# A mixture of experts on one core: gate/up rows taken eight to a partition, gathers from the plain rows, places by falling number of rows

## The reference, cut to what matters

```
def swiglu(x, w_gu, w_down):
    gate, up = jnp.split(x @ w_gu, 2, axis=-1)
    return (jax.nn.silu(gate) * up) @ w_down
...
        tok, wt, ex = inp
        y = swiglu(x_pad[tok], w_gu[ex], w_down[ex])
        return acc.at[tok].add((y * wt[:, None]).astype(acc.dtype)), None
```

## Time and profile before

| | |
|---|---|
| median of 3 runs | 2564.52 us (2564.05 to 2569.41) |
| the profiled execution | 2562.0 us, span of the trace 2560.0 us |
| PE busy, of the span | 2439.3 us (95%) |
| DVE, ACT, POOL busy | 900.5, 423.2, 793.3 us |
| moved by DMA | 391.36 MB in 167964 packets |
| places and spill loop | about 1677 to 2512 us of the span |

### The profile page before, as it was taken

One profiled execution on the slowest core, in us unless ns is written; L12 is line 12 of the kernel. 1 busy time (PEld: TensorE's weight loads), 2 busy tenths in 40 slices (PEclk: granted clock), 3 DMA queues, 4 the chain that ended last, 5 costly groups with the idle time before them and its releaser, 6 DMA issues. The chain is left out here.

```text
span 2560.0 us, 26577 instructions
## 1 busy us (share of the span) xinstructions
PE 2439.3 (95%) x10446; PEld 1480.8 (58%) x10446; DVE 900.5 (35%) x1540; ACT 423.2 (17%) x665; POOL 793.3 (31%) x764
## 2 busy tenths in 40 slices
PE   6999999999999999999999999979999999999991
PEld 3444554345799544444445544457777777776761
DVE  5011553675533532323323262222222223323325
ACT  1001122335454110010001110001111111111110
POOL 3000111101343100000001135326666666676642
PEclk9999999999999999999999999989999999999996
DMA  6201003100000211111050501079999999999995
GB/s 250 90 33 45 22 33 104 41 17 9 1 1 26 91 49 49 32 43 49 25 206 25 188 30 50 26 291 349 343 343 345 347 345 349 342 345 347 348 321 165
DMA packets 167964, 391.36 MB, mean 153 GB/s; under 512 B 19706, under 2 KB 40234, under 8 KB 167072
## 3 DMA queue, kind: packets, MB, share of 16 engines
q1 hardware_dynamic: 135248, 300.64, 32.2%
q0 software_dynamic: 31584, 82.00, 12.3%
q10 hardware_dynamic: 1008, 7.02, 0.7%
HBM read 322.50 MB, written 67.11 MB: 152 GB/s over the span
## 5 line engine op out<-in xcount | busy, mean ns | idle before, releaser
L1856 PEld LDWEIGHTS banks<-arena 128*128 128x128 f32 x4096 | 523.8, 192 | 75.8 <-DMA arena<-in_exp_w_gu 39.4
L1856 PE MATMUL banks<-arena 128*128 128x128 f32 (+7 forms) x4096 | 533.8, 292 | 30.8 <-DMA arena<-in_exp_w_gu 28.4
L2276 POOL DMA_INDIRECT arena<-hp_scratch,arena x306 | 294.8, 964 | 243.6 <-issue 80.2
L1380 PE MATMUL banks<-arena 128*128 128x512 f32 x672 | 291.8, 594 | 1.3 <-PEq L736 1.3
L328 PE MATMUL banks<-arena 128*128 128x512 f32 x640 | 280.9, 596 | 4.6 <-DVE arena L1093 4.3
L1864 PE MATMUL banks<-arena 128*128 128x512 f32 (+1 forms) x528 | 237.4, 592 | 1.4 <-DVE arena L2240 0.9
L1380 PEld LDWEIGHTS banks<-arena 128*128 128x128 f32 x672 | 127.8, 190 | 163.1 <-issue 163.1
L328 PEld LDWEIGHTS banks<-arena 128*128 128x128 f32 x640 | 120.0, 190 | 159.4 <-issue 149.7
L280 POOL TENSOR_SCALAR arena<-arena 128x1 f32<-128x1 f32 x16 | 15.5, 970 | 604.6 <-DVE arena L271 604.6
L2291 POOL DMA_INDIRECT acc_scratch<-arena x99 | 153.7, 1552 | 66.8 <-DMA acc_scratch<-arena 42.1
L321 PE MATMUL banks<-arena 128*128 128x512 f32 x384 | 168.4, 597 | 0.6 <-PE banks L321 0.6
(11 more groups left out here) (364 smaller groups left out, 2517.4 us busy)
## 6 DMA issues: line engine op xcount, KB each, us to landing
arena<-in_exp_w_gu SPq DMA_DIRECT2D x64, 2048.0 KB, 24.6
arena<-in_exp_w_down SPq DMA_DIRECT2D x64, 1024.0 KB, 20.2
arena<-in_w_in SPq DMA_DIRECT2D x10, 2048.0 KB, 9.3
arena<-in_w_in SPq DMA_DIRECT2D x12, 1024.0 KB, 6.2
arena<-in_w_branch SPq DMA_DIRECT2D x12, 512.0 KB, 7.2
hp_scratch<-arena SPq DMA_DIRECT2D x10, 512.0 KB, 2.9
arena<-hp_scratch,arena POOLq DMA_INDIRECT x306, 6.3
arena<-in_x SPq DMA_DIRECT2D x4, 1024.0 KB, 14.8
```

The costliest lines, as they stand in the source:

```text
L1380: last = nc.tensor.matmul(PS[:, g % 4, :], lhs[:, k, :], rhs[:, k, :], start=(k == 0), stop=(k == 3))
L1856: last = nc.tensor.matmul(PS[:, bank + part, f * n:(f + 1) * n], weights[:, k, part * FF + f * P:part * FF + (f + 1) * P], x[:, k, 0:n], s ...
L2276: nc.gpsimd.indirect_dma_start(out=rows[0:n, :], out_offset=None, in_=table, in_offset=bass.IndirectOffsetOnAxis(ap=at, axis=0)).then_inc( ...
```

## The change

- The gate/up matrix is loaded with rows 8p to 8p + 7 on partition p. They follow each other in memory, 16 KB in one piece.
- The token's row then needs no permutation: quarter q of the plain row, read with the eight numbers of a partition together, fits. The gathers read `hx_scratch`; the permuted copies, their stores, waits and the scratch `hp_scratch` go.
- DVE's transposes read each 32 x 32 block with a step of 8 numbers (32 bytes) from one to the next, where they read neighbours before. In the spill loop PE's eight transposes read with the same step.
- `place_order` sorts by falling capacity: 216, 216, 192, 192, 176 x4, 168 x8, 152 x8, 144 x8, 136 x4, and then all 27 single places; the spill loop stays last.

```diff
 def place_order():
-    double = [r for r in range(NE - 1) if rank_rows(r) > P]
-    single = [r for r in range(NE - 1) if rank_rows(r) == P]
-    at = {r: (i + 0.5) / len(double) for i, r in enumerate(double)}
-    at.update({r: i / (len(single) - 1) for i, r in enumerate(single)})
-    return sorted(range(NE - 1), key=lambda r: (at[r], r)) + [NE - 1]
+    return sorted(range(NE), key=lambda r: (-rank_rows(r), r))
...
-                    sp.dma_start(hp_d[pads, :], zero).then_inc(pads_in, 16)
...
-        gu_v = a["exp_w_gu"].rearrange("e (k p) n -> e p k n", p=P)
-        hq_d = hp_d.rearrange("s (q c) -> (s q) c", q=4)
+        gu_v = a["exp_w_gu"].rearrange("e (p k) n -> e p k n", p=P)
+        hq_d = hx_d.rearrange("s (q c) -> (s q) c", q=4)
...
-                def permuted_out(t):
-                    sp.wait_ge(o_perm, t + 1)
-                    sp.dma_start(hp_d[t * P:(t + 1) * P, :], hp[t % 2]).then_inc(o_sp[t % 2], 16)
-
-                for t in range(NT - 2):
-                    permuted_out(t)
                 sp.wait_ge(o_job, 2 * NT)
...
-                permuted_out(NT - 2)
-                permuted_out(NT - 1)
                 sp.wait_ge(o_n, NT)
...
-                        last = nc.tensor.transpose(PS[:, k // 4, (k % 4) * P:(k % 4 + 1) * P], xg_spill[:, k * P:(k + 1) * P], ident)
+                        last = nc.tensor.transpose(PS[:, k // 4, (k % 4) * P:(k % 4 + 1) * P], xg_spill[:, k:D:KD], ident)
...
-                    if j:
-                        act.wait_ge(o_n, t + 1)
-                        if t >= 2:
-                            act.wait_ge(o_sp[t % 2], 16 * (t // 2))
-                        nc.scalar.activation(hp[t % 2].rearrange("p (q c j) -> p q c j", q=4, c=QC),
-                                             h[:, t, :].rearrange("p (c q j) -> p q c j", q=4, c=QC), ACT.Copy).then_inc(o_perm, 1)
...
-                    src = rows[r % 2][:, 0:n * QD].rearrange("p (g c j) -> p g c j", g=n, j=32)
+                    src = rows[r % 2][:, 0:n * QD].rearrange("p (g j c) -> p g c j", g=n, j=32)
...
-                for i in range(2):
-                    pool.wait_ge(o_sp[i], 8 * NT)
```

More of the change, by code:

```diff
@@ L186, in build @@
         hx_d = nc.dram_tensor("hx_scratch", (SEQ + PADR, D), F32).ap()
-        hp_d = nc.dram_tensor("hp_scratch", (SEQ + PADR, D), F32).ap()
         gt_d = nc.dram_tensor("gt_scratch", (SEQ + PADR, NE), F32).ap()
@@ L486, in _ @@
                 act.wait_ge(a_par, 32)
-                act.wait_ge(pads_in, 144)
+                act.wait_ge(pads_in, 112)
                 def lru_evacuate(job):
@@ L1528, in build @@
         up = [carve(HALF, R2 + i * HALF) for i in range(2)]
-        hp = [carve(D, CONSTS["level"][0] + i * D) for i in range(2)]
-        assert CONSTS["level"][0] + 2 * D <= CONSTS["ranks"][0]
         wg = carve(KD * D, base).rearrange("p (j k n) -> p j k n", j=2, k=KD)
@@ L1575, in build @@
                                     "capacity", "cols", "rows", "tables", "pos"))
-        o_perm, o_sp = sem("o_perm"), [sem(f"o_store_perm{i}") for i in range(2)]
         e_slots = [sem(f"e_slots{i}") for i in range(2)]
@@ L2263, in _ @@
                     nc.gpsimd.tensor_tensor(hs, hs, up[q % 2], ALU.mult).then_inc(f_hid, 1)
-                pool.wait_ge(pads_in, 144)
+                pool.wait_ge(pads_in, 112)
                 pool.wait_ge(e_pos, 1)
```

## The result

The changed kernel takes 2568.45 us (median of 22 runs, 2565.77 to 2573.34) where the kernel before takes 2563.86 (22 runs beside it): 1.0018 times, 95% interval 1.0012 to 1.0024. One of the 22 runs of the kernel before took 3279.85 us, from a cause that is not known; the median hardly feels it. The forecast was 2556 with a range of 2545 to 2588: the time lies in the range, but on the other side of no change. The profiled execution of the changed kernel is its slowest, 2573.34 us with a span of 2571.4, against 2562.0 and 2560.0 before. So the two traces differ by 11.4 us where the medians differ by 4.6; what made that one execution longer than its median is not known, and sums over the traces are read with that in mind.

A forecast was written before the change was run, and what follows sets the result against it. PE was taken as the bound, with full DMA engines beside it in the experts. Start -5.5, late weights -11.0 (3 left over falls away), adds +8 give -8.5: 2553.5 us, median 2.5 higher: 2556, range 2545 to 2588.

The forecast's parts named there:

- The start: At the first places, a longer hidden(0) fills 4.5 us of the matrix wait and the matrix lands sooner: -5.5 us.
- Late weights: In the expert places after the start, PE's waits for late gate/up matrices go: -11.0 us, with 3 us left over.
- the overlap: In single places, adds setting 10.9 us a place cut DMA's deficit to 0.7 us, so 3 us of lateness fall away.
- Adds in single places: Adds slowed by 16 KB packets make each of 27 single places 0.3 us longer than PE needs: +8 us.
- The signs named for being wrong: Adds landing above 11 us with POOL waiting, single places at 11.5 us or more, transposes at 2.5 us, late-starting gathers.
- The mixture: In single places, q0's packets wait 0.32 us on average among q1's packet sizes, so an add lands in 10.8 us.
- rival 1: In single and the last 20 double places, adds become the chain, landing at 11.5 us: +32 us, 2580; chance 0.22.
- Copies, stores: In the stage before 1677 us, dropping ACT's permuted copies and the stores is worth 0, since PE doesn't wait for them.
- Transposes: DVE's strided transposes take 0.4 us more each, 0.8 at most, hidden behind hidden(r+1): 0 in the sum.
- Rival 2: Gains cancel: adds land at 10.8 us, costing +14 to +17 instead of +8; 2562 to 2565 us; chance 0.18.
- Rival 3: Gate/up pieces stay at 2 KB, so only the order changes; 16 us of late weights, 2565 us; chance 0.05.
- Rival 4: Whole matrices take a turn on the engines, delaying adds by 5 us or more; 162 us slower, 2726; chance 0.05.

The follow-up runs named there:

- e2: The kernel before with the new place_order alone; 2577.69 us, 1.0039 times the kernel before.
- e3: The changed kernel with each gate/up matrix loaded in four transfers, so packets are 4 KB; 2564.26 us, 0.9992 times the kernel before.
- e4: The changed kernel with the adds of odd places going to a second sum that the output leaves out; 2551.23 us, 0.9946 times the kernel before.
- e7: The changed kernel with transposes reading 32 neighbouring columns again, on a lower-clock chip; 2669.17 us, 0.9972 times the kernel before there.
- e17: The kernel before with transposes reading every eighth column, on a lower-clock chip; 1.0000 times the kernel before.
- e15: The kernel before, unchanged, run again with its own profile on a lower-clock chip; 0.9997 times the kernel before.
- e13: The changed kernel with the old place order and each gate/up matrix in four transfers (4 KB packets), on a lower-clock chip; 1.0119 times the kernel before.

## Why the prediction went wrong, step by step

- **The start** was forecast at -5.5 us. Measured -6.2 in the profiled executions. The steps were right, but a transpose that was costed as hidden takes 2.5 us of TensorE at `hidden(0)`, where no earlier `hidden` covers it; since TensorE then waits for the matrix of place 1 anyway, it costs nothing.
- **Late weights**, -11.0 us and 3 us left over, the 3 falling away where adds set the pace. Measured -11.0: no late matrix after the start. The sum was right, for the reason given under the overlap. One reading under it was off: a place of 144 rows was put at 12.3 us on PE, where its rows give 8.29 + 3.44 + 0.99 - 0.17 = 12.5 us (and the changed kernel's chain 8.04 + 3.43 + 0.98); that is DMA's own 12.5, and nothing in the sum hangs on it. That the deficit behind it was real, e2 and e3 show: 23.3 and 12.1 us of late matrices after the start.
- **Adds in single places**, the step that failed. The text took a landing of "some 10.2 us" and 0.3 us over TensorE for each of 27 places, +8 us. Measured: a landing of 11.04 to 12.16 us and a chain that is 1.08 us over TensorE in each of 21 places, 22.7 us; TensorE itself idles for 14.0 us of that stretch and for more before and behind it. In the profiled executions TensorE's last matmul ends 11.3 us later than before, so with -6.2 and -11.0 all waits on adds are worth some 28 us there; by the medians, whose difference is 6.8 us smaller, some 22. e4 takes away 18 us of it, which shows that the serial adds are the cause. The signs named for being wrong came: a landing above 11 us with POOL waiting in each single place, and single places over 11.5 us.
- **Why it was mis-sized.** The turn was right (0.59 us a packet of 16 KB, forecast 0.61, taken one for one), and so was the start, some 5 us to the first packet in e3 and in the changed kernel. The mixture was taken as an average over the place, as if q1's packets met an add at random. They do not: SP issues the matrix 1.2 us behind the down matrix, when `down` ends (2283.34 and 2284.51 us), and the add goes out when the last one has landed, both once a place and at the same distance, so each add meets the same stretch. In the add issued at 2278.06 us the first half of the packets' time is beside 16 KB packets, 0.16 MB in 2 us where e3 moves 0.30, and the second half is not. That is about 1 us of the 1.9 by which an add is longer than in e3; the other 0.9 us isn't located. The prediction had 10.8 us for the average mixture and 13.2 us next to 16 KB throughout; it went below both, to 10.2, for the cover named next.
- **A cover that was argued away.** "q1 is empty a third of the time once PE is the pace" was held against rival 1. It is so (66.5% of the engines' time in 2215 to 2465 us), and it helped only half of each add: q1 has 92.3% of the engines in the two microseconds before the first packet (2281 to 2283 us), 60.7% in the first half of the packets' time and 20.5% in the second.
- **Copies, stores**: 0, and nothing in the trace speaks against it. **Transposes**: 0.4 us taken, bound 0.8, measured 0.78 us, the upper end; hidden as the text said except at the start, by e7 and e17. The Trainium skill's note on cachelines ("SBUF — State Buffer", Door 1) pointed the right way; the trace gives it its figure, 2026 ns for 1245.
- **Rivals.** Rival 1 is what happened in kind: POOL waits on `acc_scratch` in each place, and the landing of 11.3 us is nearly its 11.5. Its price was 1.2 us in 27 places, +32, for 2580 us; with the 22 us that the medians give it would have been 2570. Rival 2, with the same mechanism at 10.8 us, came to 2562 to 2565: nearer in number, 3 to 6 us too low against 12 too high, but with too short a landing. That the measured time lies in the range at all is owed to the upper end, which was set by rival 1 and not by the forecast. Rival 3 is out: the packets are 16 KB. Rival 4 is out: 19 packets of q0 beside 16 of q1 in a microsecond are no whole matrices. By that, the rule of the Trainium skill ("DMA: Bandwidth & Descriptors", arbitration) again does not fit unless a recorded packet is one descriptor.
- **The order**: rival 3 put a single place with 2 KB at 12.1 us and a lateness of 16 us; e2 has 11.4 us and 23.3, so the deficit was put too high (0.8 and not 1.5 us a place) and the lead too.

## What to carry to other kernels

Before a transfer's packets are made larger, look for a serial chain of small transfers on another queue, and ask when in the period the two meet; an average over the period says little when both come once in each period at the same distance. Where such a chain stands, break it (a second destination, e4: 18 us) before shortening its links (e3: 0.0026 or 7 us). And sorting work by size saves a resource its switches, but puts all the pieces with the same bound side by side, so that no slack of a neighbour is left to borrow.

## What was not expected of the hardware

- On four of the chips the kernel before took 2643 to 2677 us for its 2564, at a granted clock of 0.97 for 0.984. In e15 TensorE had run without a gap and at 1.00 from 1720 to 1800 us; after that its mean is 0.95, made of stretches at 1.00 (2.4 GHz) and short ones at 0.50 (1.2 GHz), each behind some microseconds of gaps between matmuls that no wait explains. In kernels of the old order with a matrix in 4 or 8 transfers the mean was 0.90 to 0.93. The ratio of two kernels thus depends on the chip: in e13 the waits on adds are nearly gone as forecast, and it is 1.2% slower.
- A scatter-add of 64 rows takes only 1.3 us less than one of 128 (10.2 us apart against 11.6), because the rows left out are those that had the engines nearly to themselves; some 5 us of either pass before the first packet.
- Two scatter-adds under way at once take 13.5 us each for 11.3, and the places still follow one another faster.
- A transpose on VectorE that reads with a step of 32 bytes takes 2026 ns for 1024 columns, without the step 1245.
